# Unscaled exponentials, shares applied to the outputs, joined keys and a band mask on VectorE in the second attention

## What is computed

```python
# window heads (8 query heads on 2 key heads), |key - query| <= 128, with a sink
s_loc = jnp.einsum('bnqkgd,bnjkd->bnkgqj', qb, kb).astype(jnp.float32) * scale
s_loc = jnp.where(mask, s_loc, -jnp.inf)
s_ctx = jnp.einsum('bnqkgd,bjkd->bnkgqj', qb, k_ctx).astype(jnp.float32) * scale
p = jax.nn.softmax(jnp.concatenate([s_loc, s_ctx, sink_col], axis=-1), axis=-1)
o = (jnp.einsum('bnkgqj,bnjkd->bnqkgd', p_loc, vb)
     + jnp.einsum('bnkgqj,bjkd->bnqkgd', p_ctx, v_ctx))
...
# neighbourhood heads: own keys and values, relative bias, a mask of columns
s_loc = jnp.einsum('bnqhd,bnjhd->bnhqj', qb, kg).astype(jnp.float32) * scale + bias
s_loc = jnp.where(jnp.asarray(mask)[:, None], s_loc, -jnp.inf)
p = jax.nn.softmax(jnp.concatenate([s_loc, s_ctx], axis=-1), axis=-1)
...
x_new = x + g1 * _merge(o_a, o_b, on_a[l], on_b[l], w_out[l])   # rms norm of each half, product
h2 = _modulate(_rms_norm(x_new, norm2_g[l]), sh2, sc2)
x_new = x_new + g2 * _swiglu(h2, w_gate[l], w_up[l], w_down[l])
```

## Time and profile before

| | us |
|---|---|
| median of 3 runs | 819.42 |
| lowest and highest | 817.73, 819.96 |
| the profiled execution, its own time | 819.99 |
| its span in the profile | 818.2 |
| the second attention, first scores to last values | 519.6 to 598.3 |
| what follows (projection, normalisation, MLP) | 598.3 to 818.2 |

### The profile page before, as it was taken

One profiled execution on the slowest core, in us unless ns is written; L12 is line 12 of the kernel. 1 busy time (PEld: TensorE's weight loads), 2 busy tenths in 40 slices (PEclk: granted clock), 3 DMA queues, 4 the chain that ended last, 5 costly groups with the idle time before them and its releaser, 6 DMA issues. The chain is left out here.

```text
span 818.2 us, 14415 instructions
## 1 busy us (share of the span) xinstructions
PE 752.5 (92%) x5881; PEld 551.5 (67%) x5881; DVE 453.9 (55%) x820; ACT 321.0 (39%) x563; POOL 39.4 (5%) x31
## 2 busy tenths in 40 slices
PE   8999999899998998767868899898999999999998
PEld 5978976554745754543635687656547888888886
DVE  3899755544542233022130796589667766577665
ACT  4667333410442233031240854566542533434431
POOL 1000021010000000000000033100010000000000
PEclk9999999999999999999899999999999999999999
DMA  8894459979899999999999995500008354565201
GB/s 282 288 355 158 152 211 397 333 271 347 327 402 400 407 403 408 402 404 409 403 404 403 401 264 201 205 2 2 1 1 287 137 194 154 185 228 205 103 1 51
DMA packets 130501, 208.40 MB, mean 255 GB/s; under 512 B 7909, under 2 KB 55302, under 8 KB 130318
## 3 DMA queue, kind: packets, MB, share of 16 engines
q1 hardware_dynamic: 129518, 205.39, 68.9%
q10 hardware_dynamic: 864, 2.18, 0.8%
q0 software_dynamic: 64, 0.05, 0.0%
HBM read 206.51 MB, written 1.08 MB: 254 GB/s over the span
## 5 line engine op out<-in xcount | busy, mean ns | idle before, releaser
L2608 DVE TENSOR_TENSOR unit_parts<-ring,unit_parts 128x2048 fp32r<-128x2048 f32 x33 | 75.5, 2289 | 57.2 <-ACT unit_parts L1936 57.2
L1936 ACT ACTIVATE unit_parts<-ring 128x2048 fp32r<-128x2048 f32 x33 | 62.9, 1912 | 73.9 <-PE psa L1313 43.0
L1312 PE MATMUL psv<-column_parts,unit_parts 128*128 128x512 f32 (+1 forms) x192 | 65.5, 389 | 1.6 <-DVE arena L2686 1.4
L1312 PE MATMUL psa<-column_parts,unit_parts 128*128 128x512 f32 (+1 forms) x192 | 65.1, 388 | 0.0
L1020 PE MATMUL psv<-ring,arena 128*32 128x256 f32 x976 | 54.5, 380 | 0.2 <-DMA ring<-in_w_up_dram 0.2
L1313 PE MATMUL psv<-column_parts,unit_parts 128*128 128x256 f32 (+1 forms) x192 | 52.0, 271 | 0.0
L1313 PE MATMUL psa<-column_parts,unit_parts 128*128 128x256 f32 (+1 forms) x192 | 52.0, 271 | 0.0
L2729 POOL TENSOR_TENSOR small<-small,consts 128x2 f32<-128x2 f32 (+4 forms) x15 | 28.2, 1883 | 472.7 <-DVE small L2460 246.2
L954 PE MATMUL psa<-arena 128*128 128x128 f32 x224 | 34.2, 325 | 14.4 <-DMA arena<-in_w_in_dram 14.2
L1020 PEld LDWEIGHTS psv<-ring,arena 128*32 128x32 f32 x976 | 30.8, 110 | 21.0 <-DMA ring<-in_w_up_dram 0.7
L954 PEld LDWEIGHTS psa<-arena 128*128 128x128 f32 x224 | 33.1, 238 | 15.5 <-DMA arena<-in_w_in_dram 15.2
(11 more groups left out here) (436 smaller groups left out, 1726.9 us busy)
## 6 DMA issues: line engine op xcount, KB each, us to landing
ring<-in_w_gate_dram SPq DMA_DIRECT2D x43, 1024.0 KB, 9.5
ring<-in_w_up_dram SPq DMA_DIRECT2D x40, 1024.0 KB, 5.2
arena<-in_w_down_dram SPq DMA_DIRECT2D x32, 1024.0 KB
ring<-in_w_mod_dram SPq DMA_DIRECT2D x24, 1024.0 KB, 7.5
ring<-in_w_in_dram SPq DMA_DIRECT2D x23, 1024.0 KB, 10.9
ring<-in_w_down_dram SPq DMA_DIRECT2D x11, 1024.0 KB, 7.4
ring<-in_w_out_dram SPq DMA_DIRECT2D x8, 1024.0 KB, 8.1
arena<-in_w_in_dram SPq DMA_DIRECT2D x8, 512.0 KB, 12.2
```

What stands on the lines that cost most here:

```text
L1312: pe.matmul(both_parts(bank, t_0, t_1), hi, col_parts[:, :, k, t_0:t_1], start=(k == 0), stop=False)
L1936: act.activation(unit_parts[q % 3][:, 0, :], slot_of(NPRE + u_), ACT.Copy).then_inc(upper_done, 1)
L2608: vec.tensor_tensor(lo, slot_of(NPRE + at["mlp"] + 3 * n + kind), hi, ALU.subtract).then_inc(lower_done, 1)
```

## The change

The exponentials of a tile are no longer scaled. They are turned, copied and multiplied with the values as they come from ScalarE, and the outputs of eight heads are multiplied once by the shares (one over the row sums). For that, `shares` spreads eight inverted sums over 512 columns (`share_cols`), TensorE turns them (`shares_by_query`, after pairs 4, 8, 12 and 15 have been turned), ScalarE copies them out (`shares_out`), and VectorE multiplies (`outputs`); `head_squares` and the four scalings then read the product from SBUF, and the sums of squares (`head_sums2`) stand one pair later. The turns of tiles and of shares use the same two banks in alternation, by the counts `turn_at` and `shares_at`.

The keys of rows and context lie side by side (`keys_a`, `keys_b`), and scores are one product of 512 columns per tile. The band of the window heads is no longer added by TensorE, but by VectorE in place in PSUM, on 128 columns, ahead of the maximum; the constant `window_swapped` is gone. Negated maxima of a window pair are joined with the negated sinks in one small instruction, and the exponentials of eight sinks are one instruction. The table of the exponential is loaded by a `warm` activation ahead of the last head copies.

```diff
-        qaT, kaT, qbT, kbT = ar(15360, 4, T), ar(16384, 1, T), ar(16640, 4, T), ar(17664, 4, T)
-        kcaT, kcbT = ar(18688, 1, T), ar(18944, 4, T)
+        keys_a, qaT, keys_b, qbT = ar(15360, 1, 2 * T), ar(15872, 4, T), ar(16896, 4, 2 * T), ar(18944, 4, T)
+        kaT, kcaT, kbT, kcbT = keys_a[:, :, 0:T], keys_a[:, :, T:2 * T], keys_b[:, :, 0:T], keys_b[:, :, T:2 * T]
...
+        def turn_at(n):
+            return n + max(0, n - 2) // 8
+        def shares_at(k):
+            return min(8 * k + 10, NT) + k
...
                     if kind == 0:
+                        r0 = HD * (h // 4)
+                        st = [(bank[:], qaT[r0:r0 + HD, h % 4, b * P:(b + 1) * P], keys_a[r0:r0 + HD, 0, :], True, True)]
                     else:
+                        r0 = HD * (h % 2)
+                        st = [(bank[:], qbT[r0:r0 + HD, h // 2, b * P:(b + 1) * P], keys_b[r0:r0 + HD, h // 2, :], True, False)]
...
             def turn2(n):
-                pe.wait_ge(probs2_normed, n + 1)
+                pe.wait_ge(exps2_done, n + 1)
...
+            def shares_by_query(k):
+                pe.wait_ge(shares_ready, k + 1)
+                t = shares_at(k)
+                pe.wait_ge(probs2_copied, t - 1)
+                for cc in range(4):
+                    mm = pe.matmul(TB[t % 2][:, cc * P:(cc + 1) * P], share_cols[:, 2 * cc:2 * cc + 2, :], ident,
+                                   start=True, stop=True)
+                mm.then_inc(turned2_done, 1)
...
+                if p % 4 == 1 and p > 4:
+                    shares_by_query(p // 4 - 1)
...
+            pe.wait_ge(probs2_copied, shares_at(3) + 1)
             project_out(0, 1)
...
+            act.activation(warm, sink[:, 0:1], ACT.Exp, scale=0.0)
             heads_out(qbT, qnb_col)
             def head_squares(k):
-                act.wait_ge(values2_done, 8 * (k + 1))
+                act.wait_ge(heads_scaled, k + 1)
...
+            def sink_exps(k):
+                act.wait_ge(sinks_shifted, k // 2 + 1)
+                act.activation(den[:, stats_of(k)], den[:, stats_of(k)], ACT.Exp).then_inc(sink_exp_done, 1)
...
+            def shares_out(k):
+                act.wait_ge(turned2_done, shares_at(k) + 1)
+                if k >= 1:
+                    act.wait_ge(heads_scaled, k)
+                act.activation(share_rows, TB[shares_at(k) % 2][:], ACT.Copy).then_inc(probs2_copied, 1)
...
-                vec.tensor_scalar(E2[:, n % 4, :], E2[:, n % 4, :], total, None, ALU.mult).then_inc(probs2_normed, 1)
+                vec.tensor_copy(share_cols, total.unsqueeze(2).broadcast_to((P, AH, HD))).then_inc(shares_ready, 1)
...
             def outputs(k):
-                dve.wait_ge(heads_squared, k + 1)
-                vec.tensor_reduce(sqs[:, k, :], sqo[:, k % 2, :, :].rearrange("p c t -> p t c"), AX, ALU.add)
+                dve.wait_ge(values2_done, 8 * k + 8)
+                dve.wait_ge(probs2_copied, shares_at(k) + 1)
+                vec.tensor_tensor(o_scaled, PSX[k % 2][:], share_rows, ALU.mult).then_inc(heads_scaled, 1)
+                dve.wait_ge(heads_scaled, k + 1)
...
+            def head_sums2(k):
+                dve.wait_ge(heads_squared, k + 1)
+                vec.tensor_reduce(sqs[:, k, :], sqo[:, k % 2, :, :].rearrange("p c t -> p t c"), AX,
+                                  ALU.add).then_inc(heads_summed, 1)
...
+            def max2(p):
+                for n in (2 * p, 2 * p + 1):
+                    b, kind, h = tiles2[n]
+                    dve.wait_ge(scores2_done, n + 1)
+                    bank = at["SB"][n % 4]
+                    if kind == 0:
+                        far = bank[:, (1 - b) * P:(2 - b) * P]
+                        link(vec.tensor_tensor(far, far, c("window")[:, b * P:(b + 1) * P], ALU.add))
+                        ins = vec.tensor_reduce(mxt[:, n % 2:n % 2 + 1], bank[:], AX, ALU.max, negate=True)
...
                 if kind == 0:
+                    link(ins)
+                    j, h0 = stat(2 * p), tiles2[2 * p][2]
+                    vec.tensor_tensor(nm2[:, j:j + h - h0 + 1:h - h0], mxt, nsink[:, h0:h + 1:h - h0],
+                                      ALU.min).then_inc(max2_done, 2)
...
+            for p in range(NT // 2 + 4):
                 if p < NT // 2:
-                    max2(2 * p)
-                    max2(2 * p + 1)
+                    max2(p)
+                    if p % 8 == 3:
+                        shift_sinks(p // 4)
                     if p in (1, 8):
                         mask_bias(p // 8)
                     if p == 2:
                         last_gate()
-                    norm_probs(2 * p)
-                    norm_probs(2 * p + 1)
+                if p % 4 == 0 and p > 0 and p <= NT // 2:
+                    shares(p // 4 - 1)
                 if p % 4 == 2 and p > 4:
                     outputs(p // 4 - 1)
+                if p % 4 == 3 and p > 4:
+                    head_sums2(p // 4 - 1)
```

More of the change, by code:

```diff
@@ L1928, in _ @@
                     probs2(2 * p - 1)
+                if p % 4 == 1 and p > 4:
+                    shares_out(p // 4 - 1)
             def upper(q):
@@ L2571, in last_gate, with shift_sinks @@
                 vec.tensor_tensor(gv, gv, PSX[1][:], ALU.add).then_inc(last_gate_added, 1)
-            def norm_probs(n):
-                b, kind, h = tiles2[n]
-                j = stat(n)
-                dve.wait_ge(exps2_done, n + 1)
-                total = rs2[:, j:j + 1]
-                if kind == 0:
-                    link(vec.tensor_tensor(total, total, den[:, j:j + 1], ALU.add))
+            def shift_sinks(k):
+                dve.wait_ge(max2_done, 8 * k + 8)
+                vec.tensor_tensor(den[:, stats_of(k)], sink[:], nm2[:, stats_of(k)], ALU.add).then_inc(sinks_shifted, 1)
@@ L2581, in norm_probs, with shares @@
+            def shares(k):
+                dve.wait_ge(exps2_done, 8 * k + 8)
+                total = rs2[:, stats_of(k)]
+                if k % 2 == 0:
+                    dve.wait_ge(sink_exp_done, k // 2 + 1)
+                    link(vec.tensor_tensor(total, total, den[:, stats_of(k)], ALU.add))
                 link(vec.reciprocal(total, total))
-                vec.tensor_scalar(E2[:, n % 4, :], E2[:, n % 4, :], total, None, ALU.mult).then_inc(probs2_normed, 1)
+                if k >= 1:
+                    dve.wait_ge(turned2_done, shares_at(k - 1) + 1)
+                vec.tensor_copy(share_cols, total.unsqueeze(2).broadcast_to((P, AH, HD))).then_inc(shares_ready, 1)
```

91 lines of the change are left out of this document (39 added, 52 removed).

## The result

The changed kernel takes 822.99 us (median of 16 executions, 819.58 to 825.82), the kernel before 818.43 us (16 executions beside it, 817.73 to 821.70). The ratio is **1.0042 [1.0029, 1.0055]**: slower by 3.4 us. Ratios use the fast executions alone, which leaves out one of e4's eleven (1502.88 us). The prediction, 822.0 with a range of 818 to 825 and slower as the likeliest side, by 0.45 to 0.43, holds.

What follows compares the result with a forecast made beforehand. TensorE, busy nine tenths or more, was taken to bound the kernel. Stretches of -3.8 + 0.8 + 3.5 + 0.7 + 1.4 summed to +2.6 us, giving 822.0 us against the median 819.42, range 818.0 to 825.0.

Steps and rivals of the forecast that it cites:

- The rival in which the change does nothing: End of the kernel: the MLP's last transfers set it, so the change has no effect there; no chance given.
- Joined scores, 1.06: TensorE's window scores per pair fall from 1.65 to 1.06 us, neighbourhood scores from 1.86 to 1.65.
- The rival of cost in proportion to columns: Joined scores on TensorE take 1.25 us, adding 2.0 us over some ten steps: 824.0 us, chance 0.20.
- The band on VectorE: Mask add before each window maximum: 0.38 us with its link; window maxima to exponentials take 2.33 us.
- the rival of a cheap chain: Window chain on VectorE: an add of 0.25 us saves about 1.3 us, giving 820.7 us, no change; chance 0.25.
- The turns: TensorE's share turns, 1.0 us each; the first three wait 0.85, 2.6 and 0.85 us for ScalarE's copy.
- The faster rival: Waits ahead of the first three share turns vanish and the add is cheap: 816.4 us, chance 0.12.
- The opening: Start of attention until pair 4's scores end, at 536.7 against 540.42 us, with the table load hidden: -3.8 us.
- three steps at 3.69 ... other waits 0.2: From the end of pair 4's scores to pair 8's: 16.2 us with the first share turn, against 15.4: +0.8.
- S(8) to S(12): End of pair 8's scores to pair 12's: sums, bias mask and shares delay VectorE, TensorE stands 2.6 us: +3.5.
- S(12) to S(15): End of pair 12's scores to pair 15's: 13.5 us against 12.9, with the third share turn: +0.7 with rounding.
- The tail: Last values to GpSimd's power: 4.1 to 4.5 us instead of 2.7; power and VectorE's adds set MLP start: +1.4.

Runs made afterwards that it cites:

- e4: Kernel before, with only the exponential's table loaded early by one activation ahead of the last head copies; 818.00 us, ratio to before 0.9988.
- e1: Changed kernel with the first three turns of the shares and their copies one pair later; 818.46 us, ratio to before 1.0006.
- e3: Changed kernel with two unused 128x512 products filling TensorE's idle ahead of the first values; 822.60 us, ratio to before 1.0042.
- e2: Changed kernel with VectorE's two bias masks moved behind the maxima of pairs 2 and 5; 820.13 us, ratio to before 1.0019.
- e6: Changed kernel with only the last turn of shares moved ahead of the last values; 821.62 us, ratio to before 1.0025.
- e7: Kernel before with early table load and bias masks moved ahead of the first maxima and behind pair 5; 814.74 us, ratio to before 0.9956.
- e5: Changed kernel with first three share turns later, bias masks moved, last share turn ahead of the last values; 816.32 us, ratio to before 0.9962.
- e8: Kernel before with joined keys alone, one 512-column score product per tile, band still on TensorE; 817.97 us, ratio to before 0.9986.
- e11: Kernel before with early table load, moved bias masks and joined keys, tiles still scaled one by one; 814.65 us, ratio to before 0.9941.

## Why the prediction was right, and where not

- **What bounds the kernel.** Right: what the attention and the tail lost reached the end. From the turn of the normalised rows on, the two traces differ by 0.2 us. The rival in which the change does nothing is out.
- **Joined scores, 1.06.** Right: 545.55 to 546.61 for a joined group, 1.65 with mask products (545.55 to 547.20). The rival of cost in proportion to columns needed 1.25 and is refuted by the same row; that it had given 824.0, near the profile's figure, is chance.
- **The band on VectorE.** I took 0.38 with its link, between bounds of 0.25 and 0.68; it is 0.291, and 0.33 from start to start (554.69 to 555.02). The formula of the Trainium skill, "VectorE: DVE Perf Modes", in its TRN2 errata, gives an estimate of 0.29 for 128 columns, and the trace agrees, in place in PSUM too. M(8) to X(8) is 2.26 (554.69 to 556.95) against 2.33; the rival of a cheap chain needed 2.07 and falls.
- **The turns.** Right in place, releaser and size: idle of 0.81, 2.30 and 0.81 ahead of Q(0), Q(1) and Q(2) where 0.85, 2.6 and 0.85 were forecast, each released by ScalarE's copy. The faster rival said that these would be covered; they are not in this order of the code. e1 shows that its idea was sound: one place later in TensorE's list two of them vanish.
- **The opening.** Its end was right (S(4) ended at 17.45 us after S(0), forecast 17.1, and e1 with a full clock has 16.97); 536.7 against 540.42 is -3.7, though, not the -3.8 of the sum. **The step that failed** is what comes next, "three steps at 3.69 ... other waits 0.2" for S(4) to S(8). It took the granted clock for 1.00 after the opening, since the earlier trace rows and the profile before showed nothing else. In the profiled execution the clock fell behind the wait for V(0), T(1) and S(3) took 1.65 us longer. The wait of 1.16 us that e1 has ahead of V(1) took up most of that at first, so that S(4) ended only 0.5 later; then ScalarE's copy, late by the whole of it, left a wait of 1.25 ahead of V(2). 16.2 and 1.25 are the 17.47 measured. e1 and e3, with a full clock there, have V(2) at 17.06 us after S(0), where the changed kernel has 18.70 and the prediction 17.1. That the idle caused the fall isn't shown; the same idle stands in e1 and e2 without one.
- **S(8) to S(12).** +3.2 against +3.5; the sums behind ScalarE's square held VectorE (1.44 idle ahead of 553.74) as said, and e2 shows 1.55 of the wait ahead of Q(1) to be the bias mask. (For S(12) to S(15), 13.5 against 12.9 is +0.6; it was entered as +0.7, and the two roundings cancel.)
- **The tail.** Size right, 1.5 against 1.4, the path half wrong. The power started 4.6 us after the last V (604.91 against 600.29), next to the forecast's 4.1 to 4.5. But it isn't the power that held the adds. It took 0.70 us where the earlier trace rows has 2.67, and the first add of the projection still started only at 607.58: ahead of it stands VectorE's split of a weight unit (605.37, 2.29 us), which waited for ScalarE's (603.45), which now stands behind ScalarE's later square (602.91). So the moved outputs held the splits, and those held the adds; e6 shows 0.85 of the 1.5 to be the place of Q(3). Nor was 2.67 the power's own time. VectorE's split stands beside it there, and the second power of the same kernel, of the same shape and with no split beside it, takes 0.69. VectorE and GpSimd of the kernel before:

```profile
601.07 2.28 DVE L2608 TENSOR_TENSOR unit_parts<-ring,unit_parts 128x2048 fp32r<-128x2048 f32 x1
...
612.01 0.69 POOL L2729 TENSOR_TENSOR small<-small,consts 128x2 f32<-128x2 f32 x1 [8.11 <-DVE small L2600]
```

- **Against the median.** The forecast was counted from 819.42, the median of three executions; over 16 it is 818.43. The difference of the two kernels was forecast as 2.6 and is 3.4 [2.4 to 4.5]. In the trace it is 3.8, and 2.2 without the 1.64 us by which V(2) came later than in e1 with its full clock; so most of the gap between forecast and measurement may be the clock, if it falls in most executions, which isn't shown. That the absolute times lie within 1.0 us is in part luck, as the start of S(0) alone differs by up to 2.8 us between traces.

What stays open: how often the clock falls in the opening of the changed kernel. It did in its profile and in those of e6 and e7, and not in those of e1, e2 and e5, although e1, e2 and e5 had the same idle of 2.25 ahead of V(0); e7 had only 1.45. So how much of the median is owed to it, out of 0 to 1.65 us, isn't settled.

## What to carry to other kernels

Less work on engines that wait is worth nothing by itself: here 14 us less on VectorE and 128 passes less on TensorE came with a slower kernel, since the first three turns of the shares stood where their bank wasn't free, and the new adds in VectorE's chain, on which TensorE waits in window pairs. Ask of each added step what it waits for at the place where it is written, and try it one step later in the list; that one edit took back 3 us. Look at long one-off steps (a mask of 2.2 us, a table load of 1.28) before rewriting the loop: moving them in the old kernel (e7, 0.44%) gained as much as the new scheme with the same moves (e5, 0.38%).

## What the hardware showed

- The granted clock of TensorE after an idle of 2.25 us isn't the same in every execution: 0.72 and 0.71 (changed kernel), 0.62 and 0.81 (e6) in the two stretches behind it, or 1.00 (e1, e2, e5) behind the same idle. Behind 1.45 us it was 0.64 and 0.79 in e7, and 1.00 in the kernel before and in e4. In e3 it fell to 0.56 behind another gap of 2.30. A profile with a full clock doesn't promise one for a changed order of work.
- GpSimd's first power on 128x2 behind the attention took 2.67 us in the kernel before, e4, e7, e8 and e11, where VectorE's split of a weight unit (2.28 us on 128x2048) had started 0.16 us ahead of it; the power ended 0.55 us behind the split. In the changed kernel and all its variants the power started ahead of the split and took 0.70. So GpSimd stood still while VectorE's split ran, as far as the two times tell; no run moved the split alone.
- A spread of eight numbers over 512 columns on VectorE takes 0.43 us where the scaling of 512 columns takes 0.49.
